# Retention layer: the gated head output transposed by VectorE blocks and a DRAM scratch instead of by TensorE

## The chip, the core and the metric

The kernel runs on one core of a Trainium2 chip. The core has a matrix engine (TensorE, PE in the profile), two engines for elementwise work (VectorE or DVE, ScalarE or ACT), a general one (GpSimd, POOL) and SyncE (SP), which here does nothing but issue DMAs. The metric is the device time of one execution in microseconds; 666.4 us is the median of three runs of the kernel before (666.35 to 667.74).

## What is computed

Two decoder layers on 256 tokens of width 1024. Layer 0 mixes the tokens by attention, layer 1 by retention, and each is followed by an MLP with a squared ReLU. The change lies in layer 1's mixer, of which the reference reads, cut:

```python
q, k, v, g = jnp.split(h @ w_in, [D_MODEL, 2 * D_MODEL, 4 * D_MODEL], axis=-1)
...
y = retention_chunkwise(...)                       # 4 heads, 512 values per token and head
y = y * lax.rsqrt(jnp.mean(y * y, axis=-1, keepdims=True) + EPS)
y = y.transpose(0, 2, 1, 3).reshape(B, S, 2 * D_MODEL).astype(h.dtype)
return (jax.nn.silu(g) * y) @ w_out                # z = silu(g) * y, 256 x 2048
```

The product with `w_out` contracts over the 2048 features of z. TensorE contracts over partitions, so z, which is made with tokens on the partitions, is needed with features on the partitions.

## The kernel before, in words

All of it is f32. Each weight matrix comes as chunks of 1 MB (128 partitions x 2048) into a ring of four slots (`raw`). ScalarE copies a slot into a rounded high part `hi` (line 773), VectorE subtracts to get the low part `lo` (line 1004), and TensorE does three matmuls for each tile, high x high, high x low and low x high (lines 489 to 491): 24 matmuls of 512 columns for a chunk over the two halves of 128 tokens.

There is no scheduler: each engine runs the list written in its own function, and the engines meet at semaphores. What sets the order around the change:

- SP issues the load of chunk n as soon as `lo` of chunk n-4 is done (line 346), one after another from one queue.
- ScalarE splits a chunk once its slot of `hi` is free (TensorE has used the chunk four before) and the load has landed. The splits run three chunks ahead of TensorE (`split_ahead`).
- Retention runs over 4 heads h, and each head over 4 chunks (h, 0) to (h, 3): the first two give the head's values v, the last two its gate g. Head 0 stands alone, heads 1 to 3 are a loop. In a head TensorE does chunks 0 and 1, the scores (lines 730 and 734), chunks 2 and 3, and then y into the PSUM banks `scr[1]` and `scr[2]`. ScalarE turns g into silu(g) in the tile `sg` (line 970) and squares y (line 978). VectorE scales and multiplies into `sg`, which then holds z (line 1315), one instruction for each half t of the tokens.
- z of head h-1 is transposed in head h. `z_transposes` puts four TensorE transposes of 128x128 between the scores and chunk 2 (t = 0), and four between chunks 2 and 3 (t = 1), into the bank `scr[3]`. ScalarE copies the bank to `zT_hi` (line 934, `store_zT`), VectorE subtracts to get `zT_lo` (line 1277, `z_lo`). Both have that work ahead of their splits of chunks (h+1, 1) and (h+1, 2).
- z of head 3 is transposed behind chunks 1 and 2 of the 8 chunks of `w_out`. These run in the order of `WOUT_ORDER`, so that the features of head 3 (kg = 3) are first needed by the seventh chunk.

Of the kernel before, what the change touches and what calls it, by code (L numbers as in the profile page):

```python
# [28 lines left out]
F32 = mybir.dt.float32  # L29
# [6 lines left out]
P = 128  # L36
# [7 lines left out]
HR = 4  # L44
# [134 lines left out]
def program(nc, x_in, tables, a_w_qkv, a_w_o, r_w_in, r_w_out, mlp_w1, mlp_w2,  # L179
            out):  # L180
    rope_a, rope_r, decay, causal, gcol_src, ident_src, xT_src = tables
    with ExitStack() as ctx:
        def sb(name, shape, dt=F32):
            return ctx.enter_context(nc.sbuf_tensor(name, shape, dt))

        def sem(name):
            return ctx.enter_context(nc.semaphore(name))
# [8 lines left out]
        stage_a = sb("stage_a", [P, 2, 512])  # L196
        stage_b = sb("stage_b", [P, 2, 512])

        decay_sb = sb("decay_sb", [P, HR, 384])
# [113 lines left out]
        z_ready = sem("z_ready")  # L313
        zTp_ready = sem("zTp_ready")
        zT_hi_ready = sem("zT_hi_ready")
# [27 lines left out]
        def _(sp):  # L343
# [53 lines left out]
            with sp.Fori(0, 2) as i:  # L397
                for s in range(RING):
                    load(i + C_QK // 4, s, feat_view, qk_w[i * 4 + s])
            with sp.Fori(0, HR) as h:  # L400
                for s in range(RING):

                    load(h + C_VG // 4, s, tok_view, vg_w[h + (4 if s < 2 else 8), s % 2])
            for c, (n, kg) in enumerate(WOUT_ORDER):
                load(C_WOUT // 4 + c // 4, c % 4, tok_view, wout_w[n, kg])
            load_w1(1)
# [75 lines left out]
        def _(pe):  # L482
# [229 lines left out]

            def z_transposes(h, t):

                pe.wait_ge(z_ready, h * 2 + (t + 1))
                pe.wait_ge(zT_ready, h * 2 + (t + 1))
                for a in range(4):
                    m = nc.tensor.transpose(scr[:, 3, a * P:(a + 1) * P],  # L718
                                            sg[:, t, a * P:(a + 1) * P], ident[:])
                m.then_inc(zTp_ready, 1)  # L720

            def head(h, first):
# [10 lines left out]
                for half_d in range(2):  # L733
                    m = nc.tensor.matmul(scr[:, 0, SEQ:384], k_cur[:, half_d, P:SEQ],
                                         qk_r[:, bass.ds(h, 1), half_d, P:SEQ].rearrange("p a t -> p (a t)"),
                                         start=half_d == 0, stop=half_d == 1)
                m.then_inc(sr_ready, 1)
                if not first:
                    z_transposes(h - 1, 0)
                token_form(h + C_VG // 4, 2, 2, h * 4 + (B_VG + 2), 2, hT,  # L740
                           between=lambda kg: z_transposes(h - 1, 1) if not first and kg == 0 else None)
                pe.wait_ge(sT_ready, h + 1)
# [14 lines left out]
            for c, (n, kg) in enumerate(WOUT_ORDER):  # L757
                pe.wait_ge(zT_ready, 1 + 2 * (kg + 1))
                token_chunk(C_WOUT // 4 + c // 4, c % 4, kg == 0, kg == 3, 4 * kg, B_WOUT + 2 * n,
                            2 * n, (zT_hi, zT_lo),  # L760
                            after=lambda t: z_transposes(HR - 1, c - 1) if c in (1, 2) and t == 1 else
                            transpose_x(3, range(4)) if c == 7 and t == 0 else None)
            transpose_x(3, range(4, KD))
# [4 lines left out]
        def _(act):  # L768
# [163 lines left out]
            def store_zT(h, t):  # L932
                act.wait_ge(zTp_ready, h * 2 + (t + 1))
                nc.scalar.activation(zT_hi[:, bass.ds(h * 4, 4), t * P:(t + 1) * P],
                                     scr[:, 3, :].rearrange("p (a t) -> p a t", t=P),
                                     ACT.Copy).then_inc(zT_hi_ready, 1)

# [47 lines left out]
            for c in range(8):  # L985
                split_ahead(C_WOUT // 4 + c // 4, c % 4)
                if c in (1, 2):
                    store_zT(HR - 1, c - 1)
            norm_hi(3, range(KD))
# [4 lines left out]
        def _(dve):  # L994
# [3 lines left out]
            dve.sem_inc(aT_ready, 2)  # L998
            dve.sem_inc(zT_ready, 1)

# [273 lines left out]
            def z_lo(h, t):  # L1274
                dve.wait_ge(zT_hi_ready, h * 2 + (t + 1))
                k = bass.ds(h * 4, 4)
                nc.vector.tensor_tensor(zT_lo[:, k, t * P:(t + 1) * P],
                                        scr[:, 3, :].rearrange("p (a t) -> p a t", t=P),
                                        zT_hi[:, k, t * P:(t + 1) * P].bitcast(F32),
                                        ALU.subtract).then_inc(zT_ready, 1)  # L1280

            def head(h, first):
# [31 lines left out]
                for t in range(TT):  # L1314
                    nc.vector.scalar_tensor_tensor(sg[:, t, :], scr[:, 1 + t, :], small[:, 22 + t:23 + t],
                                                   sg[:, t, :], ALU.mult, ALU.mult).then_inc(z_ready, 1)

            def own_r(instruction, h, k):
# [8 lines left out]
            for c in range(8):  # L1327
                if c < 7:
                    split_ahead(C_WOUT // 4 + c // 4, c % 4)
                if c in (1, 2):  # L1330
                    z_lo(HR - 1, c - 1)
                if c == 6:
                    update_x(2, 0, C_WOUT + 6, 0, TOK_WOUT)
# [73 lines left out]
```

## Time and profile before

| | |
|---|---|
| median of three runs | 666.4 us (666.35 to 667.74) |
| the profiled execution's span, first to last instruction | 665.3 us |
| TensorE busy | 659.8 us (99%) |
| VectorE, ScalarE busy | 423.6 us (64%), 332.1 us (50%) |
| granted TensorE clock | 1.000 over the whole span |
| DMA | 123.00 MB, mean 185 GB/s |
| retention heads and w_out | about 336 to 483 us of the span |

The span is taken from one profiled execution; it is 1.1 us below the median of the runs, which is what lies around the span. Matmul durations in the trace overlap: a matmul of 512 columns is shown as 0.39 us, but the next one starts 0.23 us later. What a matmul costs in a row of them is read from the distance of the starts.

### The profile page before, as it was taken

The numbers are of one execution on the slowest core, as the hardware profiler recorded it, in microseconds if no ns is written. First come the engines' busy times: TensorE is split into PE (matmuls) and PEld (weight loads), VectorE is DVE, ScalarE is ACT, GpSimd is POOL, SyncE is SP. The second block draws the span as 40 slices with busy tenths as digits, with TensorE's granted clock in tenths as the row PEclk, the third lists the DMA queues.
The fourth block names the chain that finished last, engine by engine and source line by source line (L and its number), as shares of the span: only waits on it lengthen the run. The fifth ranks groups of instructions, "written<-read, shape, count | busy, mean of one in ns | idle before, by whom it ended". The sixth has DMA issues, their size and how long they took to land.

```text
span 665.3 us, 8894 instructions
## 1 busy us (share of the span) xinstructions
PE 659.8 (99%) x3296; PEld 557.4 (84%) x3296; DVE 423.6 (64%) x469; ACT 332.1 (50%) x435; POOL 26.8 (4%) x29
## 2 busy tenths in 40 slices
PE   8999999999999999999999999999999999999998
PEld 7888888888888888888888888888888888888887
DVE  6898666877776454459875555654478777744541
ACT  6877655655554334364446455454365555533320
POOL 0163000000000000000000000000000000000000
PEclk9999999999999999999999999999999999999999
DMA  9965456766555555535665455356637665556600
GB/s 316 388 225 186 134 163 226 224 198 190 195 191 203 190 190 188 191 127 191 193 210 167 144 172 188 126 169 185 206 113 221 190 184 189 191 197 206 195 1 32
DMA packets 82125, 123.00 MB, mean 185 GB/s; under 512 B 2352, under 2 KB 43824, under 8 KB 82096
## 3 DMA queue, kind: packets, MB, share of 16 engines
q1 hardware_dynamic: 81808, 121.28, 56.7%
q0 software_dynamic: 288, 1.31, 0.5%
q8 instruction: 20, 0.33, 0.2%
q14 instruction: 9, 0.07, 0.0%
HBM read 121.54 MB, written 1.05 MB: 184 GB/s over the span
## 4 chain that ended last, share of the span: by engine, by line
PE 99%; DVE 0%; issue 0%; DVEq 0%
PE acc L585 22%; PE acc L489 19%; PE acc L491 19%; PE acc L490 19%; PE acc L588 11%; PE scr L599 1%; PE acc L533 1%; PE acc L612 1%; PE acc L536 1%; PE scr L491 1%; PE scr L489 1%; PE scr L490 1%; PE acc L542 1%; PE scr L625 1%; PE scr L718 1%; PE scr L636 1%
## 5 line engine op out<-in xcount | busy, mean ns | idle before, releaser
L1004 DVE TENSOR_TENSOR lo<-raw,hi 128x2048 fp32r<-128x2048 f32 x108 | 247.3, 2290 | 115.9 <-ACT hi L773 115.8
L773 ACT ACTIVATE hi<-raw 128x2048 fp32r<-128x2048 f32 x108 | 207.0, 1918 | 129.9 <-PE acc L491 127.8
L585 PE MATMUL acc<-h_both,hi 128*128 128x512 f32 x640 | 223.1, 395 | 0.0
L588 PE MATMUL acc<-h_both,lo 128*128 128x256 f32 x640 | 177.8, 278 | 0.0
L585 PEld LDWEIGHTS acc<-h_both,hi 128*128 128x128 f32 x640 | 120.1, 188 | 28.1
L588 PEld LDWEIGHTS acc<-h_both,lo 128*128 128x128 f32 x640 | 120.3, 188 | 0.0
L489 PE MATMUL acc<-hi,aT_hi 128*128 128x512 f32 x252 | 98.1, 389 | 0.0
L491 PE MATMUL acc<-hi,aT_lo 128*128 128x512 f32 x252 | 98.1, 389 | 0.0
L490 PE MATMUL acc<-lo,aT_hi 128*128 128x512 f32 x252 | 98.0, 389 | 0.0
L489 PE MATMUL acc<-hi,h_both 128*128 128x512 f32 x208 | 83.6, 402 | 0.0
L491 PE MATMUL acc<-hi,h_both 128*128 128x512 f32 x208 | 81.2, 391 | 0.0
L490 PE MATMUL acc<-lo,h_both 128*128 128x512 f32 x208 | 81.0, 390 | 0.0
L491 PEld LDWEIGHTS acc<-hi,aT_lo 128*128 128x128 f32 x252 | 47.3, 188 | 9.9
L489 PEld LDWEIGHTS acc<-hi,aT_hi 128*128 128x128 f32 x252 | 47.3, 188 | 9.8
L490 PEld LDWEIGHTS acc<-lo,aT_hi 128*128 128x128 f32 x252 | 47.3, 188 | 9.7
L904 ACT COPY stage_a<-acc 128x512 f32<-128x512 f32 x32 | 18.7, 586 | 72.6 <-PE acc L588 72.6
L491 PEld LDWEIGHTS acc<-hi,h_both 128*128 128x128 f32 x208 | 39.0, 188 | 8.4
L490 PEld LDWEIGHTS acc<-lo,h_both 128*128 128x128 f32 x208 | 39.1, 188 | 7.7
L489 PEld LDWEIGHTS acc<-hi,h_both 128*128 128x128 f32 x208 | 39.1, 188 | 7.5
L1215 DVE TENSOR_TENSOR stage_a<-acc,stage_a 128x512 f32<-128x512 f32 x32 | 22.1, 691 | 22.7 <-ACT stage_a L904 22.7
L1218 DVE SCALAR_TENSOR_TENSOR stage_a<-stage_a 128x512 f32<-128x512 f32 x32 | 22.2, 693 | 5.5 <-DVE stage_a L1215 1.9
L489 PE MATMUL acc<-hi,zT_hi 128*128 128x512 f32 x64 | 25.2, 393 | 0.0
(130 smaller groups left out, 585.9 us busy)
## 6 DMA issues: line engine op xcount, KB each, us to landing
raw<-in_mlp_w SPq DMA_DIRECT2D x64, 1024.0 KB, 5.4
raw<-in_r_w_in SPq DMA_DIRECT2D x24, 1024.0 KB, 5.1
raw<-in_a_w_qkv SPq DMA_DIRECT2D x8, 1024.0 KB, 9.9
raw<-in_r_w_out SPq DMA_DIRECT2D x8, 1024.0 KB, 4.9
raw<-in_a_w_qkv SPq DMA_DIRECT2D x16, 256.0 KB, 6.5
raw<-in_a_w_o SPq DMA_DIRECT2D x4, 1024.0 KB, 5.1
x<-in_x SPq DMA_DIRECT2D x1, 1024.0 KB, 12.2
decay_sb<-in_decay POOLq DMA_DIRECT2D x1, 768.0 KB, 6.6
```

Source lines behind the costliest of these rows:

```text
L489: nc.tensor.matmul(dst, a_hi, b_hi, start=first, stop=False)
L490: nc.tensor.matmul(dst, a_hi, b_lo, start=False, stop=False)
L491: return nc.tensor.matmul(dst, a_lo, b_hi, start=False, stop=last)
L533: nc.tensor.matmul(acc[:, t, :], hT_hi[:, k, tokens[t]], w_hi, start=k == 0, stop=False)
L536: nc.tensor.matmul(acc[:, t, :], hT_lo[:, k, tokens[t]], w_hi, start=False, stop=False)
L585: nc.tensor.matmul(bank, feat_view(hi, s)[:, kt, o * P:(o + 1) * P], h_both[:, kt, :, :].rearrange("p b t -> p (b t)"), start=kt == 0, sto ...
L588: m = nc.tensor.matmul(bank[:, 0:SEQ], feat_view(lo, s)[:, kt, o * P:(o + 1) * P], hT_hi[:, kt, :], start=False, stop=kt == KD - 1)
L773: nc.scalar.activation(hi[:, s, :], raw[:, s, :], ACT.Copy).then_inc(hi_ready, 1)
L904: nc.scalar.copy(sq, pair).then_inc(cross_ready, 1)
L1004: nc.vector.tensor_tensor(lo[:, s, :], raw[:, s, :], hi[:, s, :].bitcast(F32), ALU.subtract).then_inc(lo_ready, 1)
L1215: nc.vector.tensor_tensor(sq, pair, sq, ALU.add).then_inc(dv.sem, 1)
L1218: nc.vector.scalar_tensor_tensor(sq, sq, 0.0, sq, ALU.max, ALU.mult).then_inc(sq_ready, 1)
```

## The change

VectorE, having made z of a head in `sg`, transposes each half in blocks of 32x32 into the tile `z_blocks` (the memory of `stage_a`, not used in the heads). SP writes the blocks to a DRAM tensor `z_rows`: four DMAs for each half t, one for each group of 32 partitions, in runs of 128 elements (512 B). When they have landed it reads each half back with one DMA of 128x512 elements into `zT_raw` (the memory of `stage_b`), in which partition d then holds feature d of all the tokens. ScalarE and VectorE make `zT_hi` and `zT_lo` from that tile in SBUF in place of the PSUM bank. The TensorE transposes and their semaphore are gone. For head 3 the two engines do that work one chunk later than before.

```diff
+    z_rows = nc.dram_tensor("z_rows", (HR, TT, P, 4, P), F32, kind="Internal").ap()
...
+        z_blocks, zT_raw = stage_a, stage_b
...
-            with sp.Fori(0, HR) as h:
+            def turn_z(h):
+                for t in range(TT):
+                    sp.wait_ge(z_blocks_ready, TT * h + t + 1)
+                    for i in range(4):
+                        rows = z_rows[h, t].rearrange("(j r) i c -> i r j c", j=4)[i]
+                        sp.dma_start(rows, z_blocks[32 * i:32 * i + 32, t, :].rearrange("p (j c) -> p j c", j=4)
+                                     ).then_inc(z_out[t], 16)
+                for t in range(TT):
+                    sp.wait_ge(z_out[t], 64 * (h + 1))
+                    if h > 0:
+                        sp.wait_ge(zT_ready, TT * (h - 1) + t + 1)
+                    sp.dma_start(zT_raw[:, t, :], z_rows[h, t].rearrange("d i c -> d (i c)")).then_inc(z_in[t], 16)
+
+            for h in range(HR):
                 for s in range(RING):
+                    if h >= 2 and s == 3:
+                        turn_z(h - 2)
                     load(h + C_VG // 4, s, tok_view, vg_w[h + (4 if s < 2 else 8), s % 2])
             for c, (n, kg) in enumerate(WOUT_ORDER):
+                if c % 4 == 3:
+                    turn_z(HR - 2 + c // 4)
                 load(C_WOUT // 4 + c // 4, c % 4, tok_view, wout_w[n, kg])
...
-                if not first:
-                    z_transposes(h - 1, 0)
-                token_form(h + C_VG // 4, 2, 2, h * 4 + (B_VG + 2), 2, hT,
-                           between=lambda kg: z_transposes(h - 1, 1) if not first and kg == 0 else None)
+                token_form(h + C_VG // 4, 2, 2, h * 4 + (B_VG + 2), 2, hT)
+                if not first:
+                    pe.wait_ge(z_ready, h * 2)
...
             def store_zT(h, t):
-                act.wait_ge(zTp_ready, h * 2 + (t + 1))
+                act.wait_ge(z_in[t], h * 16 + 16)
...
+                for t in range(TT):
+                    dve.wait_ge(z_ready, h * 2 + (t + 1))
+                    if not first:
+                        dve.wait_ge(z_out[t], h * 64)
+                    nc.vector.transpose(z_blocks[:, t, :].rearrange("p (j a c) -> p a j c", j=4, a=4),
+                                        sg[:, t, :].rearrange("p (a j c) -> p a j c", a=4, j=4)
+                                        ).then_inc(z_blocks_ready, 1)
```

The order of instructions on TensorE in the loop body of heads 1 to 3, from the last scores matmuls to the first matmul of chunk (h, 2), before:

```order
L734 MATMUL scr<-qk_r,k_cur 128x128
L734 ISA
L734 MATMUL scr<-qk_r,k_cur 128x128
L715 ISA
L718 MATMUL scr<-ident,sg 128x128 [waits zT_ready,z_ready]
L718 MATMUL scr<-ident,sg 128x128 x3
L486 REGISTER_ALU
L501 REGISTER_ALU [waits lo_ready]
L489 MATMUL acc<-hi,h_both 128x512 [waits acc_free]
```

and the same place of the changed kernel:

```order
L749 MATMUL scr<-qk_r,k_cur 128x128
L749 ISA
L749 MATMUL scr<-qk_r,k_cur 128x128
L510 REGISTER_ALU
L525 REGISTER_ALU [waits lo_ready]
L513 MATMUL acc<-hi,h_both 128x512 [waits acc_free]
```

The four transposes and their two waits are gone; nothing takes their place. The same holds between chunks (h, 2) and (h, 3) and behind chunks 1 and 2 of `w_out`; ahead of y of heads 1 to 3 stands a new wait for z of the head before.

SP at the end of the loop over heads (the loads of the chunks (h, 2) and (h, 3)) and at the loads of `w_out`, before:

```order
L347 DMA raw<-in_r_w_in 128x4x512
L346 REGISTER_ALU
L347 ISA [waits lo_ready]
L347 DMA raw<-in_r_w_in 128x4x512
L400 REGISTER_ALU
L400 COMPARE_AND_BRANCH
L347 DMA raw<-in_r_w_out 128x4x512 [waits lo_ready] x8
```

and the changed kernel from the first load of a head to the second turn of z (the 11 loads are those of heads 0 and 1 and (2, 0) to (2, 2)):

```order
L353 DMA raw<-in_r_w_in 128x4x512 [waits lo_ready] x11
L413 DMA z_rows<-stage_a 32x4x128 [waits z_blocks_ready]
L413 DMA z_rows<-stage_a 32x4x128 x3
L413 DMA z_rows<-stage_a 32x4x128 [waits z_blocks_ready]
L413 DMA z_rows<-stage_a 32x4x128 x3
L419 DMA stage_b<-z_rows 128x512 [waits z_out0]
L419 DMA stage_b<-z_rows 128x512 [waits z_out1]
L353 DMA raw<-in_r_w_in 128x4x512 [waits lo_ready] x4
L413 DMA z_rows<-stage_a 32x4x128 [waits z_blocks_ready]
```

The turn of a head's z, ten DMAs with three kinds of waits, stands between two weight loads: turn 0 ahead of the load of (2, 3), turn 1 ahead of (3, 3), turns 2 and 3 ahead of chunks 3 and 7 of `w_out`.

VectorE at the end of the loop body, from z of head h to the splits behind the loop, before:

```order
L1315 SCALAR_TENSOR_TENSOR sg<-scr,small,sg 128x512 [waits dve_step]
L1315 SCALAR_TENSOR_TENSOR sg<-scr,small,sg 128x512
L1323 REGISTER_ALU
L1323 COMPARE_AND_BRANCH
L1004 TENSOR_TENSOR lo<-raw,hi 128x2048 [waits hi_ready] x2
```

and now:

```order
L1328 SCALAR_TENSOR_TENSOR sg<-scr,small,sg 128x512 [waits dve_step]
L1328 SCALAR_TENSOR_TENSOR sg<-scr,small,sg 128x512
L1334 REGISTER_ALU [waits z_ready]
L1335 STREAM_TRANSPOSE stage_a<-sg 128x4x4x32 [waits z_out0]
L1335 STREAM_TRANSPOSE stage_a<-sg 128x4x4x32 [waits z_out1,z_ready]
L1344 REGISTER_ALU
L1344 COMPARE_AND_BRANCH
L1016 TENSOR_TENSOR lo<-raw,hi 128x2048 [waits hi_ready] x3
```

Two transposes of 128x512 elements are added for each head, ahead of the split of the next head's chunk 3.

## Rows read from the trace of the kernel before

**Rows 1.** Page, part 1: busy us (share of span) x instructions, by engine.
```profile
PE 659.8 (99%) x3296; PEld 557.4 (84%) x3296; DVE 423.6 (64%) x469; ACT 332.1 (50%) x435; POOL 26.8 (4%) x29
```
**Rows 2.** Page, part 4: chain that ended last, by engine.
```profile
PE 99%; DVE 0%; issue 0%; DVEq 0%
```
**Rows 3.** Windows (length, busy PE PEld DVE ACT POOL, clock, DMA, GB/s): heads' scores to y.
```profile
347.33:359.57 12.24, 12.24 (x57) 10.21 (x56) 7.01 (x6) 6.92 (x6) 0.00 (x0) 1.00 0.54 171
372.49:385.61 13.12, 13.12 (x65) 11.05 (x64) 8.31 (x8) 6.59 (x7) 0.00 (x0) 1.00 0.49 160
398.53:411.65 13.12, 13.12 (x65) 11.04 (x64) 8.31 (x8) 6.60 (x7) 0.00 (x0) 1.00 0.49 160
424.57:437.69 13.12, 13.12 (x65) 11.05 (x64) 8.31 (x8) 6.59 (x7) 0.00 (x0) 1.00 0.46 160
...
361.61:387.65 26.04, 26.04 (x122) 21.75 (x121) 14.71 (x15) 13.58 (x16) 0.69 (x1) 1.00 0.48 155
```
**Rows 4.** Timeline of PE, w_out: start us, us, engine, line, operation, tiles, count.
```profile
439.73 0.39 PE L489 MATMUL acc<-hi,zT_hi 128*128 128x512 f32 x1
...
450.62 0.60 PE L718 MATMUL scr<-ident,sg 128*128 128x128 f32 x4
450.97 0.48 PE L489 MATMUL acc<-hi,zT_hi 128*128 128x512 f32 x1
...
456.55 0.60 PE L718 MATMUL scr<-ident,sg 128*128 128x128 f32 x4
...
462.46 0.39 PE L489 MATMUL acc<-hi,zT_hi 128*128 128x512 f32 x1
```
**Rows 5.** Groups by line and form: busy us, mean ns, then idle before, releaser.
```profile
L718 PE MATMUL scr<-ident,sg 128*128 128x128 f32 x32 | 4.8, 272 | 0.0
L1142 DVE TENSOR_SCALAR probs<-probs,small 128x256 f32<-128x256 f32 x8 | 2.8, 347 | 0.0
```
**Rows 6.** Timeline of DVE from z of head 0 into head 1.
```profile
363.90 1.41 DVE L1315 SCALAR_TENSOR_TENSOR sg<-scr,small,sg 128x512 f32<-128x512 f32 x2
365.23 2.28 DVE L1004 TENSOR_TENSOR lo<-raw,hi 128x2048 fp32r<-128x2048 f32 x1
369.20 2.29 DVE L1004 TENSOR_TENSOR lo<-raw,hi 128x2048 fp32r<-128x2048 f32 x1 [1.69 <-ACT hi L773]
374.11 0.56 DVE L1287 TENSOR_TENSOR sT<-scr,decay_sb 128x384 f32<-128x384 f32 x1 [2.62 <-PE scr L734]
...
376.61 0.68 DVE L1277 TENSOR_TENSOR zT_lo<-scr,zT_hi 128x512 f32 x1
```
**Rows 7.** Timeline of ACT in heads 1 and 2.
```profile
375.14 0.58 ACT L934 ACTIVATE zT_hi<-scr 128x512 f32 x1
375.62 1.91 ACT L773 ACTIVATE hi<-raw 128x2048 fp32r<-128x2048 f32 x1
380.43 0.60 ACT L934 ACTIVATE zT_hi<-scr 128x512 f32 x1 [2.91 <-PE scr L718]
...
388.44 0.61 ACT L943 COPY k_cur<-qk_r 128x512 f32 x1
388.95 1.92 ACT L773 ACTIVATE hi<-raw 128x2048 fp32r<-128x2048 f32 x1
```
**Rows 8.** Line 347, weight loads from SP: durations of the issue, then time to landing.
```profile
L347 SPq DMA_DIRECT2D raw<-in_r_w_in x24: 372/373/378, 255.4 to 393.7; - x24
...
DMA to landing us min/median/max: 4.8/5.1/14.0
```
**Rows 9.** Timeline of SP: the load of chunk (2, 3).
```profile
367.68 0.37 SPq L347 DMA_DIRECT2D raw<-in_r_w_in  x1
```
**Rows 10.** DMA issues from 640 us on: writes to DRAM, KB each, us to landing.
```profile
out_x<-x SPq DMA_DIRECT2D x1, 256.0 KB, 2.0
out_x<-x SPq DMA_DIRECT2D x2, 128.0 KB, 1.7
```

More of the change, by code:

```diff
@@ L313, in program @@
         z_ready = sem("z_ready")
-        zTp_ready = sem("zTp_ready")
+        z_blocks_ready = sem("z_blocks_ready")
+        z_out = [sem(f"z_out{t}") for t in range(TT)]
+        z_in = [sem(f"z_in{t}") for t in range(TT)]
         zT_hi_ready = sem("zT_hi_ready")
@@ L711, in _ @@
                 wide_feature_form(C_QK // 4 + c // 4, c % 4, B_QK + 2 * c)
[L713 to L720, printed above, removed]
             def head(h, first):
@@ L757, in _ @@
             for c, (n, kg) in enumerate(WOUT_ORDER):
-                pe.wait_ge(zT_ready, 1 + 2 * (kg + 1))
+                pe.wait_ge(zT_ready, 2 * (kg + 1))
                 token_chunk(C_WOUT // 4 + c // 4, c % 4, kg == 0, kg == 3, 4 * kg, B_WOUT + 2 * n,
                             2 * n, (zT_hi, zT_lo),
-                            after=lambda t: z_transposes(HR - 1, c - 1) if c in (1, 2) and t == 1 else
-                            transpose_x(3, range(4)) if c == 7 and t == 0 else None)
+                            after=lambda t: transpose_x(3, range(4)) if c == 7 and t == 0 else None)
             transpose_x(3, range(4, KD))
@@ L932, in store_zT @@
             def store_zT(h, t):
-                act.wait_ge(zTp_ready, h * 2 + (t + 1))
-                nc.scalar.activation(zT_hi[:, bass.ds(h * 4, 4), t * P:(t + 1) * P],
-                                     scr[:, 3, :].rearrange("p (a t) -> p a t", t=P),
-                                     ACT.Copy).then_inc(zT_hi_ready, 1)
+                act.wait_ge(z_in[t], h * 16 + 16)
+                nc.scalar.activation(
+                    zT_hi[:, bass.ds(h * 4, 4), t * P:(t + 1) * P].rearrange("p a (i c) -> p a i c", i=4),
+                    zT_raw[:, t, :].rearrange("p (i a c) -> p a i c", i=4, a=4), ACT.Copy).then_inc(zT_hi_ready, 1)
             def head(h, first):
@@ L986, in _ @@
                 split_ahead(C_WOUT // 4 + c // 4, c % 4)
-                if c in (1, 2):
-                    store_zT(HR - 1, c - 1)
+                if c in (2, 3):
+                    store_zT(HR - 1, c - 2)
             norm_hi(3, range(KD))
@@ L998, in _ @@
             dve.sem_inc(aT_ready, 2)
-            dve.sem_inc(zT_ready, 1)
             def split(g, s):
@@ L1276, in z_lo @@
                 k = bass.ds(h * 4, 4)
[L1277 to L1280, printed above, removed]
+                nc.vector.tensor_tensor(
+                    zT_lo[:, k, t * P:(t + 1) * P].rearrange("p a (i c) -> p a i c", i=4),
+                    zT_raw[:, t, :].rearrange("p (i a c) -> p a i c", i=4, a=4),
+                    zT_hi[:, k, t * P:(t + 1) * P].rearrange("p a (i c) -> p a i c", i=4).bitcast(F32),
+                    ALU.subtract).then_inc(zT_ready, 1)
             def head(h, first):
@@ L1329, in _ @@
                     split_ahead(C_WOUT // 4 + c // 4, c % 4)
-                if c in (1, 2):
-                    z_lo(HR - 1, c - 1)
+                if c in (2, 3):
+                    z_lo(HR - 1, c - 2)
                 if c == 6:
```

## The prediction

> **What bounds the kernel now.** I read the page's busy times first: TensorE is busy 659.8 of 665.3 us, the next engine 423.6 [rows 1]. A busy share alone says little here, since matmul records overlap, so the second view is the chain of waits that ended last: 99% of it is TensorE [rows 2]. TensorE waits for nobody in the stretch of the change either: in each of the four windows from the scores to y its busy time equals the window [rows 3]. So what TensorE issues is on the path, and what the other engines and the DMAs do is beside it as long as it stays in time. The question has two parts: what do 32 transposes cost TensorE, and does the new route of z stay beside it?
>
> **What is removed.** The 32 transposes come as 8 groups of four. Their price is a difference of like stretches. From the first scores matmul to the first y matmul head 0, which has no transposes, takes 12.24 us, and heads 1, 2 and 3 take 13.12 each with two groups: 0.88 us a head, 3 x 0.88 = 2.64 us [rows 3]. The window of head 0 has 57 matmul records and each of the others 65, so the eight transposes are the only difference. The other two groups stand in w_out: from the first one's start to the second's 5.93 us, from the second's to the next chunk 5.91 [rows 4]; a chunk without one takes 5.445 us ((450.62 - 439.73) / 2, the two chunks ahead of the first group [rows 4]). That is 0.485 + 0.465 = 0.95 us. Sum: 2.64 + 0.95 = 3.59 us, about 0.11 us a transpose. That includes the 0.1 us or so which the first matmul behind a group loses: its record is 0.48 us long and not 0.39 [rows 4].
>
> The transposes' own records say 272 ns each, 32 of them 8.7 us [rows 5], but four of them and the way to the next matmul take 450.97 - 450.62 = 0.35 us [rows 4]: a record's length contains latency that the next instruction overlaps. The Trainium skill ("TensorE: Matmul & The Clock Gate", Part 4: PE-mode transpose) gives about 275 ns for such a transpose in a kernel. The trace agrees with that as a record's length, and not as a price. By the page's figure the estimate would be a gain of 8.8 us; by the starts it is 3.6.
>
> **What is added on VectorE.** Two block transposes of 128x512 a head, behind z. No row shows such an instruction. Bounds: 0.35 us each (the 256-column SBUF pass of 347 ns [rows 5], were it twice as fast per column) and 2.29 us (a 128x2048 pass [rows 6], four times the elements). I take 0.7, as z's own pass over the same tile takes (1.41 / 2 [rows 6]). They push the split behind them from 365.23 to 366.6, its end from 367.5 to 368.9, and the next split only starts at 369.20, since it waits for ScalarE (1.69 us of idle there [rows 6]). Price 0. At 2.29 us each the two splits would end at 372.1 and 374.4, and the decay product due at 374.11 would start 0.3 us late, with y, which needs it, only due at 385.61 [rows 3]: again 0. The new reads of SBUF by ScalarE and VectorE for `zT_hi` and `zT_lo` take the place of PSUM reads that cost 0.58 and 0.68 us [rows 6, 7]; a ScalarE SBUF copy of this size took 0.61 [rows 7]. Also 0.
>
> **What is added on SP and the DMAs.** Ten DMAs a head. A weight load keeps SP 0.37 us [rows 8]; so do these, for want of another row (half of it to twice it moves the numbers below by 2 to 4 us). For head 0: z is done at 365.3 [rows 6], the blocks of t = 0 at 366.0, of t = 1 at 366.7. SP issues four writes until 367.5 and four more until 369.0. A write of 256 KB to DRAM landed in 2.0 us and one of 128 KB in 1.7 [rows 10], in rows of 2 and 1 KB; the pieces here are 64 KB in runs of 512 B. Bounds for a leg: 1.7 us, and 14.0, the longest landing among the weight loads [rows 8]. I take 2.0 each way: t = 0 landed at 369.5, read back by 371.9; t = 1 at 371.0 and by 373.4. ScalarE asks for t = 0 at 375.14 and for t = 1 behind the split, at 377.5 at the earliest [rows 7], where before it sat 2.91 us until the transposes came at 380.43. So z is there 3 to 4 us early, and ScalarE even gains slack.
>
> If it were late, ScalarE would stand at `store_zT` with the split of chunk (2, 1) queued behind it, and VectorE's `lo` of that chunk behind that. TensorE starts head 2 at 387.65, where the window of the whole head 1 ends [rows 3], and chunk (2, 1) at 387.65 + 5.44 - 0.88 = 392.2. Going back 2.29 for `lo`, 1.92 for `hi` and 0.58 for `zT_hi`, z may come as late as 387.4: 21 us after its blocks, against the 6 that I expect.
>
> The turn also stands in front of weight loads. The load of (2, 3) is issued at 367.68 [rows 9]; now SP passes the turn at about 371.4, so it lands at about 376.9 with 5.1 us of flight [rows 8]. ScalarE splits it at 388.95 - 0.88 = 388.1 [rows 7]. There are 11 us to spare. The same holds at the other three turns, since each stands at the same place of the period; for head 3 the consumer is the seventh chunk of w_out, over 20 us later. The traffic: 512 KB out and back beside 4 MB of weights a head, a quarter more. DMA's share of the whole head's window is 0.48 [rows 3] and would go to about 0.6. Price 0; the cover is this reserve of 11 to 21 us in a period of 26. The new wait of TensorE for z ahead of y finds z done some 20 us before.
>
> **Sum.** 665.3 - 3.6 = 661.7 us of span, and with the 1.1 us that lie between the span and the median of the runs, 662.8 us.
>
> **Rivals.**
> 1. *The round trip through DRAM is slow, and ScalarE's wait for it becomes the bound* (slower). The place is `store_zT` of heads 0 to 2, and it decides from 21 us after the blocks. For it: no row shows writes in 512 B runs, and the reads have to wait for the writes. Against it: the two stores at the end landed in 2 us [rows 10]. With 14.0 us for each leg t = 0 would be back at 367.5 + 14.0 + 0.4 + 14.0 = 395.9, 8.5 us late, in three heads 25 us, less the 3.6 saved: 688 us. The Trainium skill ("VectorE: DVE Perf Modes", The three transpose paths) warns that a plain DMA copy which does a transpose by strides is 19 times slower than the crossbar one. The warning is for large innermost strides; here VectorE has done the innermost part and the DMA moves runs of 512 B. No run here shows it yet; applied to the 2.0 us leg it would be an estimate of 38 us for the write, t = 0 back at 407.9, 20 us late and three times so, about 724 us.
> 2. *The extra traffic and the turn's place in SP's queue make weight loads late* and take back most of the gain. For it: two loads now leave SP at once behind a turn. Against it: 11 us to spare, DMA at half its share. Price: 2 to 3 us over the heads, 665.3 us, no measurable change.
> 3. *A transpose costs what its record says*, 272 ns: 666.4 - 8.7 = 657.7 us. Against it are the starts in rows 4 and the windows in rows 3.
> 4. *TensorE gets back only a part*, because some pause at the places of the groups was there for another reason (the switch from scores to the wide matmuls, the semaphore waits). Head 0 has the switch too and is in the comparison; only w_out's two groups have no twin. Price: without the 0.95, 663.8 us.
>
> **How the numbers follow.** The forecast has 0.82, with its own range of 662.2 to 663.4. Rival 4 has 0.05, rival 3 0.01, rival 2 0.06, rival 1 0.06 with the 0.01 of the page's version in it. A measurement of this kernel tells about 0.2%, 1.3 us, from no change. Faster by more: 0.82 + 0.05 + 0.01 = 0.88. Within: rival 2, 0.06. Slower: rival 1, 0.06. The range has to take in rival 4 and a part of rival 2, and leaves out rivals 1 and 3: 662.0 to 664.8.
>
> **What would show it.** In the changed kernel's windows from scores to y all four heads should read 12.2 us, a w_out chunk behind the first two 5.44, and the period of a head 25.16 in place of 26.04. ScalarE's `zT_hi` should start without waiting for a DMA, the block transposes should be near 0.7 us, the writes and reads should land in 2 to 3 us each. I am wrong if the waits show ScalarE held by the DMA into `stage_b` for over 12 us, or any TensorE idle time before a `hi` or `lo` in the heads, or if the block transposes take over 5.8 us each, at which `lo` of chunk (1, 3), done at 365.3 + 11.6 + 2.3 = 379.2, would come as TensorE gets to it (385.61 - 0.88 - 5.44 = 379.3).

## The result, and the profile after

| | before | changed |
|---|---|---|
| runs, median us (lowest to highest) | 667.07 (666.35 to 668.36), 4 runs | 662.95 (662.64 to 664.01), 4 runs |
| profiled execution, span us | 665.3 | 661.0 |

The ratio of the runs is 0.9933, with a 95% interval of 0.9918 to 0.9947: the change takes 4.5 us off a time of 667, by the interval between 3.5 and 5.5. The two medians in the table are 4.1 us apart. Both kernels' granted TensorE clock is 1.00 throughout. Of the experiments below, one of the two runs of `e6_blocks4` took 726.0 us at a mean granted clock of 0.852 and is left out. Faster was forecast, with 662.8 us.

Start with the busy times and the chain, as before. Columns are those of [rows 1, 2].

```profile
PE 655.6 (99%) x3264; PEld 554.3 (84%) x3264; DVE 428.1 (65%) x477; ACT 332.4 (50%) x435; POOL 26.8 (4%) x29
...
PE 99%; DVE 0%; issue 0%; DVEq 0%
```

TensorE has 32 matmuls fewer and is busy 4.2 us less, VectorE has 8 instructions more and is busy 4.5 us more. TensorE is still the whole chain, so only its side of this exchange counts.

The windows from each head's first scores matmul to its first y matmul, then the whole period of head 1's weights, answer to [rows 3]. The columns are the same: length, busy PE, PEld, DVE, ACT, POOL, clock, DMA share, GB/s.

```profile
346.60:358.84 12.24, 12.24 (x58) 10.21 (x56) 7.01 (x6) 6.92 (x6) 0.00 (x0) 1.00 0.54 171
371.76:384.00 12.24, 12.24 (x58) 10.21 (x56) 8.22 (x8) 6.67 (x7) 0.00 (x0) 1.00 0.78 277
396.92:409.16 12.24, 12.24 (x58) 10.21 (x56) 8.22 (x8) 6.67 (x7) 0.00 (x0) 1.00 0.77 277
422.08:434.32 12.24, 12.24 (x58) 10.21 (x56) 8.22 (x8) 6.67 (x7) 0.00 (x0) 1.00 0.78 274
360.88:386.04 25.16, 25.16 (x115) 20.91 (x113) 15.80 (x17) 13.66 (x16) 0.69 (x1) 1.00 0.66 209
```

Heads 1, 2 and 3 have the length of head 0, 12.24 us where it was 13.12, and the scores of the heads start 25.16 us apart (371.76 - 346.60). TensorE is busy for the whole of each window, so nothing waits in them. What grew is the DMAs' share: 0.78 in the windows that hold a turn through DRAM, where it was 0.49.

The w_out chunks on TensorE, the first matmul of each, answer to [rows 4] (start, duration, line, tiles):

```profile
436.36 0.39 PE L513 MATMUL acc<-hi,zT_hi 128*128 128x512 f32 x1
...
441.80 0.39 PE L513 MATMUL acc<-hi,zT_hi 128*128 128x512 f32 x1
...
447.24 0.39 PE L513 MATMUL acc<-hi,zT_hi 128*128 128x512 f32 x1
...
452.68 0.39 PE L513 MATMUL acc<-hi,zT_hi 128*128 128x512 f32 x1
...
458.12 0.39 PE L513 MATMUL acc<-hi,zT_hi 128*128 128x512 f32 x1
```

These are the starts of chunks 0 to 4. Each chunk takes 5.44 us, and so do chunks 2 and 3, which with their groups of transposes took 5.93 and 5.91.

Where the time came from: from the first scores matmul to the end of the span is 665.3 - 347.33 = 317.97 us before [rows 3] and 661.0 - 346.60 = 314.40 after. That is 3.57 us, good to about 0.1, since a span is given to 0.1 us. The windows say the same more sharply: three times 0.88 in the heads, and 5.93 - 5.44 and 5.91 - 5.44 in w_out, 3.60 us. The other 0.73 us of the 4.3 between the two spans lie before the heads, where no instruction of the change stands; differences of that kind are measured below.

The new route beside it. First SP behind the z of head 0: the writes, the reads back, the weight loads behind them. A row's duration runs from the first issue of the group to the end of the last, waits between them included.

```profile
365.22 3.75 SPq L413 DMA_DIRECT2D z_rows<-stage_a  x8
369.02 1.67 SPq L419 DMA_DIRECT2D stage_b<-z_rows  x2
370.73 12.66 SPq L353 DMA_DIRECT2D raw<-in_r_w_in  x4
```

The DMA issues of this part of the program: KB each, median us from issue to landing; these answer to [rows 8, 10].

```profile
z_rows<-stage_a SPq DMA_DIRECT2D x32, 64.0 KB, 1.8
stage_b<-z_rows SPq DMA_DIRECT2D x8, 256.0 KB, 3.1
```

VectorE in the same turn answers to [rows 6]:

```profile
364.50 1.29 DVE L1335 STREAM_TRANSPOSE stage_a<-sg 128x512 f32<-128x512 f32 x2
365.71 2.25 DVE L1016 TENSOR_TENSOR lo<-raw,hi 128x2048 fp32r<-128x2048 f32 x1
368.47 2.29 DVE L1016 TENSOR_TENSOR lo<-raw,hi 128x2048 fp32r<-128x2048 f32 x1 [0.51 <-ACT hi L786]
373.38 0.56 DVE L1300 TENSOR_TENSOR sT<-scr,decay_sb 128x384 f32<-128x384 f32 x1 [2.62 <-PE scr L749]
```

And ScalarE, where z comes back, answers to [rows 7]:

```profile
374.40 0.62 ACT L947 ACTIVATE zT_hi<-stage_b 128x512 f32 x1
374.92 1.90 ACT L786 ACTIVATE hi<-raw 128x2048 fp32r<-128x2048 f32 x1
376.73 0.61 ACT L947 ACTIVATE zT_hi<-stage_b 128x512 f32 x1
...
387.33 1.92 ACT L786 ACTIVATE hi<-raw 128x2048 fp32r<-128x2048 f32 x1
```

Neither `zT_hi` has a bracket, so neither waited; the second, which stood 2.91 us behind the transposes, now runs at 376.73 and not at 380.43. Note that everything in the heads comes 0.73 us earlier in this trace. The block transposes push the split behind them from 365.23 to 365.71, which with these 0.73 us is a push of 1.2, and VectorE's wait for ScalarE after it shrinks from 1.69 to 0.51 us, by the same 1.2: that idle time paid for them. The split at 387.33, of chunk (2, 3), whose load left behind the turn, waited for no DMA either.

### The profile page after: what moved, and what is told of

Its sections match the earlier page's. It is cut to its first block, busy times and chain, and to the rows that moved or that the text cites. A ratio compares the mean times of both kernels' runs of the same rounds, so it can differ in the third digit from the quotient of the medians.

```text
span 661.0 us, 8821 instructions
## 1 busy us (share of the span) xinstructions
PE 655.6 (99%) x3264; PEld 554.3 (84%) x3264; DVE 428.1 (65%) x477; ACT 332.4 (50%) x435; POOL 26.8 (4%) x29
## 4 chain that ended last, share of the span: by engine, by line
PE 99%; DVE 0%; issue 0%; DVEq 0%
PE acc L609 22%; PE acc L515 19%; PE acc L513 19%; PE acc L514 19%; PE acc L612 11%; PE scr L623 1%; PE acc L636 1%; PE scr L515 1%; PE scr L513 1%; PE scr L514 1%; PE acc L557 1%; PE acc L560 1%; PE acc L566 1%; PE scr L649 1%; PE scr L660 1%; PE scr L681 1%
```

## The experiments

The theory: TensorE is the bound and gets back the time that the transposes held it, 0.11 us each; the route costs nothing, because VectorE, ScalarE, SP and the DMAs have 11 to 21 us of reserve. The rivals: the route costs something and the transposes were worth more; their price is the record's length, or a fixed loss per group; weight loads come late. The runs of before on the chips of the experiments had medians of 667.9 us (29 runs, beside experiments 1 to 3 and the two trips), 667.3 (13, beside the four trips and experiments 5 and 6) and 668.0 (12, beside experiment 7).

**1. Neither the transposes nor the route** (`e1_no_route`, from the kernel before):

```diff
                 if not first:
-                    z_transposes(h - 1, 0)
-                token_form(h + C_VG // 4, 2, 2, ..., between=lambda kg: z_transposes(h - 1, 1) ...)
+                    pe.wait_ge(z_ready, h * 2)
...
-                act.wait_ge(zTp_ready, h * 2 + (t + 1))
+                act.wait_ge(z_ready, h * 2 + (t + 1))
...
-                                     scr[:, 3, :].rearrange("p (a t) -> p a t", t=P),
+                                     stage_b[:, t, :].rearrange("p (a t) -> p a t", t=P),
```

Expected:

> The kernel before without its 32 transposes and without any other route: zT_hi and zT_lo are made from whatever lies in stage_b, so z is not transposed and the w_out product is of the wrong data. Theory (TensorE is the bound, the new route of z is free): the same time as the changed kernel, 3.6 us below before, about 0.9946 of it; all four windows from scores to y 12.24 us. Rival (block transposes, ten DMAs a head and their waits cost something that the removal hides): over 0.5 us below the changed kernel's gain, 4.1 us or more below before.

Measured: 665.01 us (662.57 to 666.73, 12 runs), ratio 0.9957 (0.9944 to 0.9970). In its profile the four windows are 12.24 us each and the chunks of w_out 5.44. From the first scores matmul to the end it takes 662.8 - 348.46 = 314.34 us; the changed kernel takes 314.40. So in the stretch where it runs the route costs nothing that a span given to 0.1 us can show. The median, however, is 2 us above the changed kernel's. The runs of before beside it are 0.8 us slower too (667.9 for 667.07); 1.2 us remain. The trace has the place: its span is 1.8 us longer, and its first scores matmul comes 1.86 us later, at 348.46 and not 346.60. What that is stands at the end of this section.

**2. The new route and the old transposes** (`e2_both`, from the changed kernel; the transposes write PSUM that nobody reads):

```diff
+                    z_transposes(h - 1, 0)
+                token_form(h + C_VG // 4, 2, 2, ..., between=lambda kg: z_transposes(h - 1, 1) ...)
-                    pe.wait_ge(z_ready, h * 2)
```

Expected:

> The changed kernel with the 32 TensorE transposes put back at their old places, their output read by nobody. Theory: the time of before, ratio 1.000 within 0.1%, windows of heads 1 to 3 back at 13.12 us. Rival (part of the gain came from elsewhere, such as the reads from SBUF instead of PSUM or the start of the program, where TensorE's first matmuls stand 0.7 us earlier in the changed kernel's trace): 0.5 to 0.9 us below before.

Measured: 666.85 us (665.75 to 668.46, 12 runs), ratio 0.9989 (0.9976 to 1.0001). The windows of heads 0 and 1, as above:

```profile
345.98:358.22 12.24, 12.24 (x58) 10.21 (x57) 7.02 (x6) 6.92 (x6) 0.00 (x0) 1.00 0.53 171
371.15:384.27 13.12, 13.12 (x66) 11.04 (x65) 8.22 (x8) 6.67 (x7) 0.00 (x0) 1.00 0.76 263
```

The 0.88 us are back although the DMAs still carry the turn (share 0.76). From the first scores matmul to the end: 664.0 - 345.98 = 318.02 us, before 317.97. With experiment 1 this closes the square: without and with the transposes 314.3 and 318.0 us, whether z goes through DRAM or not. The medians alone would not have decided it: 666.85 is 1.05 us below the 667.9 of before, nearer to the rival than to the theory, and the interval of the ratio takes in both. The trace puts that difference ahead of the heads, as the rival did (345.98 where before has 347.33), so it is no part of what the transposes or the route cost; experiment 7 comes back to it.

**3. Each group of transposes twice** (`e3_twice`, from the kernel before):

```diff
-                for a in range(4):
+                for a in [0, 1, 2, 3] * 2:
```

Expected:

> The kernel before with each group of four transposes done twice in a row, eight in a group. Three prices: by the distance of starts, 0.35 us for four (0.0875 each) and about 0.1 once for a group, 32 more cost 2.8 us, 669.3 us (1.0042 of before); by an even share of the removed 3.59 us they cost 3.6 us, 670.1 us (1.0054); by the record's 272 ns they cost 8.7 us, 675.2 us (1.013).

Measured: 671.8 us (669.9 to 672.46, 6 runs), ratio 1.0062 (1.0044 to 1.0081). The window of head 1 is 14.03 us (12.24, 13.12, 14.03 for 0, 8 and 16 transposes), and from the first scores matmul to the end it is 667.8 - 346.22 = 321.58 us, 3.61 more than before for 32 more. TensorE's timeline at a group of eight, and the first matmul behind it:

```profile
372.68 1.04 PE L718 MATMUL scr<-ident,sg 128*128 128x128 f32 x8
373.48 0.48 PE L489 MATMUL acc<-hi,h_both 128*128 128x512 f32 x1
```

The first matmul starts 0.80 us behind the group's first transpose, 0.35 behind it with four [rows 4], so four more take 0.45. The price is even: 3.57 us for the first 32 and 3.61 for the next, 0.112 and 0.113 us each. If each group had a fixed loss, doubling the groups' size would have cost less than the first four did, 2.8 us by the first of the three prices; it didn't. The price by the records, 32 times 272 ns, would have been 8.7 us and is excluded.

**4. Two trips through DRAM, and four** (`e4_trips2`, `e5_trips4`, from the changed kernel; each trip waits for the one ahead; shown for two):

```diff
+                for trip in range(2):
+                    ...
+                        if trip > 0:
+                            sp.wait_ge(z_mid[t], ...)
```

Expected of two:

> The changed kernel with the way through DRAM done twice for each head: written, read back, written again, read back again, and only the second reading releases ScalarE. In the changed kernel's trace t = 0 of head 0 is back at about 372.1 and ScalarE asks at 374.4. A second trip adds about 7.3 us: back at 379.5, ScalarE waits 5 us in each of three heads. Theory (reserve until z delays lo of chunk (2, 1), due at 391.5, so until 391.5 - 2.29 - 1.92 - 0.61 = 386.7): the time of the changed kernel, 662.9 us. Rival (any wait of ScalarE for z reaches TensorE): 3 x 5 = 15 us more, 678 us.

Measured: 664.03 us (662.56 to 666.16, 10 runs), ratio 0.9945 (0.9930 to 0.9959). ScalarE's timeline at the return of z, and its waits for it over the whole span (us, times, longest):

```profile
378.47 0.63 ACT L952 ACTIVATE zT_hi<-stage_b 128x512 f32 x1 [4.00 <-DMA stage_b<-z_rows]
...
ACT zT_hi L952 <- DMA stage_b<-z_rows: 16.9, 4, 5.2
```

ScalarE now stands 3.8 to 5.2 us for z of each head, and TensorE doesn't notice: all windows 12.24 us, 661.0 - 346.57 = 314.43 us to the end. A wait on the new route costs nothing as long as it is shorter than the reserve. The traffic of the turns doubled as well, which speaks against rival 2, the late weight loads.

Expected of four:

> The changed kernel with four ways through DRAM for each head in place of one. With two, a further one took 6.6 us: z of head 0 was read back at 378.4, ScalarE waited 4 us and TensorE lost nothing. With four it is back at about 378.4 + 13.2 = 391.6. Theory (what counts is lo of chunk (2, 1), for which z must be back by 386.7): TensorE waits about 5 us before chunk (2, 1) in head 1. The turn of head 1 then starts late as well, since SP has the load of (3, 2) in front of it, which waits for a lo that this delay pushes back; so heads 2 and 3 lose more than the first, 10 us or so each, and the sum is 15 to 40 us above the changed kernel, 678 to 703 us. Rival (weight loads behind the turn are the bound, not ScalarE's wait): TensorE's first wait comes at chunk (2, 3) and ScalarE is then shown waiting for raw, not for stage_b.

Measured: 709.22 us (707.87 to 710.57, 2 runs), ratio 1.0626 (1.0601 to 1.0652). ScalarE, and TensorE at chunk (2, 1):

```profile
393.16 0.63 ACT L952 ACTIVATE zT_hi<-stage_b 128x512 f32 x1 [17.16 <-DMA stage_b<-z_rows]
...
397.97 0.79 PE L518 MATMUL acc<-hi,h_both 128*128 128x512 f32 x1 [4.83 <-DVE lo L1021]
```

TensorE stands where it was said to: ahead of chunk (2, 1), for VectorE's `lo`, which waits for the split that stands behind `zT_hi` on ScalarE. It came to the chunk at 397.97 - 4.83 = 393.14, 0.9 us later than the 392.2 of the prediction; 0.8 of that is that the heads start later in this trace (348.10 where before has 347.33). With the wait of 4.83 us `zT_hi`, which starts at 393.16, is 4.8 us behind a deadline of 388.3, in the prediction's own time 387.5, where it had 387.4. The waits of ScalarE for weights come to 6.6 us for the largest group, against 80.9 for z, so the bound is the wait for z. The size is a miss: 46 us over the changed kernel, above the forecast. In the heads it lost 7.3 and 12.4 us (20.21 and 25.29 us from y to the next scores, in place of 12.92), near what was forecast. More than half of the miss is w_out: from head 3's y to the end takes 708.8 - 455.48 = 253.3 us in place of 661.0 - 434.32 = 226.7. I had not costed that z of head 3 and the weights behind it in SP's queue hit w_out as well, where TensorE stood 9.76 and 8.34 us. A further part is the clock: in the two stretches from y to the scores TensorE is busy 15.4 us with the work that takes 12.92 in the changed kernel, at a mean granted clock of 0.83 and 0.80. Experiment 5 shows where it falls.

**5. Each block transpose four times, and twelve** (`e6_blocks4`, `e7_blocks12`, from the changed kernel; shown for four):

```diff
+                    for again in range(4):
+                        if again > 0:
+                            dve.wait_ge(z_again, ...)
                         nc.vector.transpose(...)
```

Expected of four:

> The changed kernel with each block transpose done four times on VectorE (with a semaphore wait between them), eight instructions a head and not two. At 0.68 us and about 0.1 for the wait they end 4.6 us later than now, lo of chunk (1, 3) at about 372.6 against TensorE's start of that chunk at 378.6, z of t = 0 back 2 us after ScalarE asks. Theory: no change of time, 663 us, windows 12.24 us. Rival (VectorE's added time reaches TensorE): 3 to 4 x 4.6 us more, 677 us or above.

Measured: 664.13 us, in one run, so there is no interval; the trace decides. VectorE:

```profile
365.83 5.77 DVE L1339 STREAM_TRANSPOSE stage_a<-sg 128x512 f32<-128x512 f32 x8
371.52 4.45 DVE L1017 TENSOR_TENSOR lo<-raw,hi 128x2048 fp32r<-128x2048 f32 x2
```

4.5 us more a head on VectorE, ScalarE waits for z once in the whole run, 0.9 us, and the windows stay at 12.24 us, the stretch to the end at 662.3 - 347.93 = 314.37. VectorE's part of the change is free with four times its size.

Expected of twelve:

> The changed kernel with each block transpose done twelve times, 24 instructions a head, about 17.8 us, beyond the limit of 5.8 us for each of two (11.6 us) that was forecast. The blocks end at about 382.3, lo of chunk (1, 3) at 384.6, TensorE wants it at 378.6. Theory: TensorE waits about 6 us ahead of chunk 3 of heads 1, 2 and 3, and up to 4 us ahead of chunk 3 of w_out: 18 to 25 us above the changed kernel, 681 to 688 us. Rival (the wait of ScalarE for z, 16 us later than now, comes first): TensorE's wait stands ahead of chunk 1 of the next head.

Measured: 699.61 us (699.27 to 699.96, 2 runs), ratio 1.0483 (1.0462 to 1.0503). VectorE, then TensorE:

```profile
366.56 17.72 DVE L1339 STREAM_TRANSPOSE stage_a<-sg 128x512 f32<-128x512 f32 x24
384.20 4.45 DVE L1017 TENSOR_TENSOR lo<-raw,hi 128x2048 fp32r<-128x2048 f32 x2
...
386.51 0.79 PE L514 MATMUL acc<-hi,h_both 128*128 128x512 f32 x1 [5.73 <-DVE lo L1017]
```

24 block transposes are 8.9 us for each of the two that the changed kernel has, over the 5.8 at which the prediction saw the limit, and TensorE stands ahead of chunk (1, 3), the place that it named. The limit can be read from it: the wait would be gone with 5.73 us less of them, at 17.72 - 5.73 = 12.0 us for two, 6.0 each where the prediction had 5.8. The loss of 37 us is again above the forecast; the windows of the same trace say why. The columns are those of [rows 3]; the first is TensorE's wait, the others the time behind it.

```profile
380.76:386.51 5.75, 0.02 (x2) 0.01 (x1) 5.61 (x7) 0.00 (x0) 0.00 (x0) 0.75 0.15 34
386.51:388.50 1.99, 1.99 (x5) 1.60 (x6) 1.99 (x1) 0.00 (x0) 0.00 (x0) 0.50 0.68 164
388.50:390.50 2.00, 2.00 (x7) 1.54 (x6) 1.94 (x4) 1.34 (x3) 0.00 (x0) 0.52 0.92 247
390.50:393.91 3.41, 3.41 (x16) 2.80 (x15) 3.03 (x3) 3.41 (x3) 0.00 (x0) 1.00 1.05 401
```

Behind a wait of 5.75 us TensorE has a granted clock of 0.50, that is 1.2 of its 2.4 GHz, for about 4 us, and then 1.00 again. The scores-to-y window of head 1 is 20.09 us, of which TensorE is busy 14.36: 12.24 us of work at full clock took 2.12 more. So a wait of 5.73 us cost 7.85. Over the three heads (20.09, 20.73, 20.87 in place of 12.24) that is 25.0 us, and w_out lost 10.2 (698.2 - 461.35 against 226.7), with one wait of 7.13 us where up to 4 were expected. The rest, 2.1 us, lies ahead of the heads, and 1.7 of it is the W1 stage of experiment 7.

**6. The same route for two more tiles** (`e8_queries`, from the changed kernel: rotated queries 4 and 5 of layer 0 turn through VectorE and DRAM as well, eight TensorE transposes fewer). It tries for a faster kernel.

```diff
+                        if i not in TURNED:
                             transpose_rot(i)
...
+                if p_i in TURNED:
+                    act.wait_ge(q_in[t], 16)
+                    nc.scalar.copy(qkT[...], q_raw[:, t, :]...).then_inc(qkT_ready, 1)
...
+            def q_turn(p_i):
+                nc.vector.transpose(z_blocks[:, t, :]..., rot[:, t, :]...).then_inc(q_blocks_ready, 1)
```

Expected:

> A version meant to be faster: the changed kernel with the same route (block transpose, eight writes, two reads) for two more groups of TensorE transposes, the rotated queries of heads 4 to 7 in layer 0's attention (two groups of four of the L625 kind), whose result is needed some 20 us later. Theory: two groups less on TensorE, 2 x 0.45 = 0.9 us below the changed kernel, 662.0 us where that takes 662.9; in the trace the way from TensorE's chunk 2 of the QKV product to the first matmul of W_o shortens by 0.9 us (68.15 us in the changed kernel). Rival (this stretch has the busiest VectorE and ScalarE and loads one after another, so the two passes on VectorE, or ScalarE's wait for the data, delay lo or the scores): no gain, or 1 to 3 us lost in that stretch.

Measured: 665.67 us (665.38 to 667.35, 8 runs), ratio to before 0.9979 (0.9967 to 0.9991), where the changed kernel has 0.9933 (0.9918 to 0.9947): slower than the changed kernel, and the rival held. The windows from TensorE's second chunk to the first W_o matmul, of the changed kernel:

```profile
16.45:84.60 68.15, 68.15 (x339) 56.81 (x337) 55.10 (x113) 51.72 (x136) 19.30 (x15) 1.00 0.70 234
```

and of this one, with the waits of TensorE in it:

```profile
17.34:87.42 70.08, 67.76 (x331) 55.78 (x329) 56.28 (x115) 51.65 (x136) 19.16 (x15) 1.00 0.71 240
...
54.45 0.33 PE L689 MATMUL scr<-ident,probs 128*128 128x128 f32 x1 [0.87 <-DVE probs L1191]
...
62.06 0.33 PE L689 MATMUL scr<-ident,probs 128*128 128x128 f32 x1 [0.92 <-DVE probs L1191]
...
69.78 0.63 PE L669 MATMUL scr<-ident,rot 128*128 128x128 f32 x4 [0.53 <-ACT qkT L885]
```

TensorE is busy 0.39 us less and idle 2.32, as three rows show, for VectorE's `probs` twice. In attention VectorE is busy 55 of 68 us, and softmax of each head hangs on it; in the heads it is busy 16 of 25 (the period of head 1, above). VectorE's rows ahead of the first of these waits:

```profile
46.12 0.71 DVE L1146 STREAM_TRANSPOSE stage_a<-rot 128x512 f32<-128x512 f32 x1
...
50.46 0.70 DVE L1146 STREAM_TRANSPOSE stage_a<-rot 128x512 f32<-128x512 f32 x1
...
53.84 0.55 DVE L1191 TENSOR_SCALAR probs<-probs,small 128x128 f32<-128x128 f32 x2
```

Between 46 and 54 us VectorE has no idle time. The changed kernel, whose stretch starts 0.89 us earlier, has the same `probs` at 51.77, so here it comes 1.2 us later: the two block transposes cost 1.4 us of an engine that had none to give at that place. The stretch takes 1.93 us longer; with the 0.89 of its later start the heads begin 2.8 us later (349.42 for 346.60), and from there to the end it takes 314.4 us as before.

**7. The changed kernel and the one without a route, on one chip** (`f1_changed_again` is the changed kernel, `f2_no_route_again` is `e1_no_route`). This was to explain the 2 us between their medians.

> The changed kernel itself, beside f2 and the kernel before on one chip. The medians so far put it 4.1 us under before (4 runs) and e1_no_route, which has no route of z at all, only 2.9 (12 runs), while the traces put both at 314.4 us from the first scores matmul on. If the route costs nothing, as the traces say, f1 and f2 have one median within 0.7 us, and both lie 3 to 4.5 us below before: ratio 0.9935 to 0.9955. If the changed kernel is really a microsecond faster than the one without the route, f1 stays a microsecond or more under f2.

> e1_no_route again (no transposes and no route: zT is split from what lies in stage_b, so z of the heads is left out of the result). If the route costs nothing: the median of f1 within 0.7 us. If something in the route makes the kernel faster elsewhere: a microsecond or more over f1.

Measured: for the changed kernel 664.12 us (662.15 to 664.58, 6 runs), ratio 0.9942 (0.9925 to 0.9958); for the other 664.90 us (664.37 to 666.05, 7 runs), ratio 0.9961 (0.9948 to 0.9975). The changed kernel's gain is there again. The distance is 0.8 us, just over the 0.7 that I had set, and the kernel without the route is again the slower one. The traces show that it is not in the stretch where the route runs: from the first scores matmul to the end `f2_no_route_again` takes 663.9 - 349.52 = 314.4 us. Windows over the W1 stages of layer 0 and layer 1 and, between them, from W2 to the heads. Of the changed kernel's first profile:

```profile
112.14:200.97 88.83, 88.83 (x515) 77.72 (x514) 70.57 (x70) 50.04 (x58) 0.71 (x1) 1.00 0.62 189
200.97:346.60 145.63, 145.22 (x707) 121.96 (x705) 89.41 (x78) 61.52 (x54) 0.70 (x1) 1.00 0.58 188
482.14:570.98 88.84, 88.84 (x516) 78.34 (x515) 70.58 (x70) 50.30 (x58) 0.69 (x1) 1.00 0.61 190
```

of the same kernel in `f1_changed_again`:

```profile
112.79:201.62 88.83, 88.83 (x516) 77.72 (x514) 70.59 (x70) 50.05 (x58) 0.71 (x1) 1.00 0.62 189
201.62:346.36 144.74, 144.33 (x706) 121.52 (x705) 89.34 (x78) 61.53 (x54) 0.70 (x1) 1.00 0.57 189
481.91:572.44 90.53, 90.53 (x515) 78.56 (x514) 70.64 (x70) 50.30 (x58) 0.70 (x1) 1.00 0.60 186
```

and of `f2_no_route_again`:

```profile
113.36:203.89 90.53, 90.53 (x515) 78.56 (x514) 70.64 (x70) 50.05 (x58) 0.71 (x1) 1.00 0.61 186
```

The same kernel, the same number of matmuls, the clock at 1.00, TensorE without a wait in either W1 stage (and idle for the same 0.41 us between them), and a stage takes 88.83 or 90.53 us, another 144.74 or 145.63. One execution may differ from the next by 1.70 us twice and 0.89 once, and by 0.7 in the start. That is enough to make medians of one gain read as 4.1, 3.9 and 2.9 us, and it is why the stretch from the heads on decides, taken apart by stage: `f1_changed_again` has 316.14 us there, 314.4 plus the 1.70 of its last W1 stage, with windows of 12.24 us and chunks of 5.44 all the same. Both profiles of the kernel without a route have the long W1 stage in layer 0, both of the changed kernel the short one. The twelve profiles of this document say that it is not the missing route that makes it long: 90.53 us stand there in five, these two and those of `e5_trips4`, `e6_blocks4` and `e7_blocks12`, which all have the route; the other seven, before among them, have 88.83. Whether some kernels have the long stage more often stays open.

A second part of the distance lies outside the spans. A run's time minus its own span is 1.74 to 1.86 us in each of the runs of the changed kernel and of all kernels made from it, and on average 2.05 to 2.13 us, group of runs by group, in those of the kernel before and of the kernels made from that one, those without a route included. So the changed kernel gains another 0.3 us which no profile shows, and which stays when the transposes are put back (`e2_both`: 1.79 us). What in the program makes it wasn't tried.

## Why the prediction was right

- **The price of the transposes** was the step that the sum rests on: 3.59 us forecast, 3.57 in the trace (3.60 by its windows), and experiments 1, 2 and 3 give 3.6 by leaving the transposes out, putting them back and doubling them. Taking like stretches of one trace (head 0 as the twin without transposes) was right; taking record lengths would have given 8.7. The Trainium skill ("TensorE: Matmul & The Clock Gate", Part 4: PE-mode transpose) has about 275 ns for one of 128x128, on a line that speaks of bf16; the records here, in f32, say 272, and the price in a row of them is 113.
- **The remark on the first matmul** behind a group, that it loses 0.1 us, adds up for a group of four: 0.35 us to its start and 0.09 of a longer record are the 0.44 that the windows give. What it led to was wrong: experiment 3 first took the 0.1 for a fixed cost of a group, with 0.0875 us a transpose beside it. Behind eight the record is 0.48 us as well, yet eight more transposes cost 0.91 us in a window, as much as the first eight (0.88). A group of four costs 0.44 us and one of eight 0.895, 0.110 and 0.112 a transpose, and nothing fixed. The sum did not depend on it.
- **w_out's two groups** gave back their 0.95 us: rival 4, a partial gain, was wrong.
- **Block transposes** at 0.7 us: they took 0.68 each. Price 0, as forecast. Experiment 5 shows the cover from both sides: free at four times, a TensorE wait at twelve, at the chunk named.
- **SP and the DMAs.** Three sizes were off. A write kept SP 0.445 us and not 0.37; it landed in 1.8 us for 2.0; the read back took 3.1 and not 2.0. The first two nearly cancel for t = 0. The third is 1.1 us: z of t = 0 was back at about 369.02 + 3.1 = 372.1, 2.3 us before ScalarE asked (374.40), where 3 to 4 were forecast. The guess of a share of about 0.6 came out at 0.66.
- **The reserve** was the argument against rival 1, and it held: with one trip more (6.6 us, the first writes of the two trips start at 365.20 and 371.82) ScalarE waits and TensorE doesn't, with three more both do, at chunk (2, 1). The rule on transposing DMA copies (the Trainium skill, "VectorE: DVE Perf Modes", The three transpose paths), which by the prediction's estimate would have made this 724 us, did not bite: writes of 64 KB in runs of 512 B landed in 1.8 us.
- **Rival 2**, late weight loads, is out: the split of chunk (2, 3) doesn't wait, and with twice the traffic of the turns nothing changed.
- **The distance to the median** is the term of the sum that was wrong. The 1.1 us came from the median of three runs and the span of one execution. Run by run, time minus span is 1.8 us in the changed kernel and about 2.1 in the one before (experiment 7). So the closeness of 662.95 to 662.8 is in part luck: the span came out 0.7 us shorter than 661.7, ahead of the heads, and the changed kernel's median lies 1.95 us above that span and not 1.1. By its own place the gain is 3.6 us; with the 0.3 outside the span that makes 3.9, beside medians that are 4.1 and 3.9 us apart.

## What to carry to other kernels

When one engine is the whole chain, price its instructions by the distance between starts in two like stretches, one with them and one without, and not by the length of their records. Work can then be moved to a longer route over other engines and DRAM for nothing, but only if its deadline on every queue that it enters is later than the route is long: here some 20 us of reserve took a turn of 6 us, and in attention, where VectorE had nothing to spare at the place, the same move lost 1.9 us in its stage. If a gain is smaller than the scatter of the runs, look for it in the stretch it belongs to.

## What the runs showed of the hardware

- A stage of alternating matmuls with 512 and 256 columns runs in one of two cadences in an execution. The W1 stage of 16 chunks with 32 matmuls each takes 88.83 or 90.53 us, 5.55 or 5.66 a chunk, with the granted clock at 1.00 in both. It is the same kernel that shows both, stage by stage (experiment 7). What decides it stays open.
- A TensorE wait of 5.73 us cost 7.85: behind it the granted clock was 0.50 (1.2 GHz) for some 4 us (experiment 5). The waits of 0.5 to 0.9 us in experiment 6 left it at 1.00.
- A 128x128 f32 transpose in a row of them costs TensorE 0.113 us (experiment 3); a 128x512 f32 block transpose costs VectorE 0.68 us, near the 0.7 of z's own pass over the tile; a trip of two such tiles (512 KB, eight writes and two reads) through DRAM takes 6.6 us (experiment 4).
